# A two-layer hybrid block: ten input chunks in one 512-column product, and softmax probabilities turned by 32x32 blocks and transfers

## The reference

```python
h = rms_norm(x, norm_mix[l])
proj = h @ w_in[l]
(dq, dk, dv, dz, da, db, mq, mk, mv, lx, ly, gates) = split_columns(proj)
# delta rule: q, k, v = split(silu(causal_depthwise_conv(concat(dq, dk, dv), conv_w)))
# recurrence: xc = causal_depthwise_conv(lx, conv_w) + conv_b
# attention, one block of 256 keys:
s = where(k_pos <= q_pos, q @ k.T * scale, -inf)
o = softmax(s) @ v
```

## Time and profile before

| | |
|---|---|
| median of 3 runs | 910.72 us |
| profiled execution | 911.29 us |
| its span | 909.5 us |
| TensorE matmul busy | 898.0 us, 99% |
| VectorE busy | 661.5 us, 73% |
| ScalarE busy | 513.9 us, 56% |
| granted TensorE clock over the span | 0.998 |
| bytes moved | 173.22 MB, 190 GB/s |

### The profile page before, as it was taken

How to read it: one execution, slowest core, us unless ns; L and a number is a source line. 1 busy time by engine, 2 the same in 40 slices (tenths; PEclk the granted TensorE clock), 3 DMA queues, 4 the chain that set the end, 5 groups by cost and what they waited for, 6 DMA issues and landing times.

```text
span 909.5 us, 13892 instructions
## 1 busy us (share of the span) xinstructions
PE 898.0 (99%) x5460; PEld 765.8 (84%) x5460; DVE 661.5 (73%) x1096; ACT 513.9 (56%) x877; POOL 2.4 (0%) x6
## 2 busy tenths in 40 slices
PE   8999999999999999999999999999999999999996
PEld 5999899788887888888879998988888888888885
DVE  6879876797968665656688797767978675665756
ACT  7586555875446444445465766568644554444443
POOL 0000000000000000000000000000000000000000
PEclk9999999999999999999999999999999999999999
DMA  8544435456664777677755344255656567767761
GB/s 308 196 157 163 146 112 162 162 197 231 206 224 158 214 200 255 201 220 250 216 179 171 117 163 138 96 181 190 229 192 205 184 215 216 252 196 231 237 202 47
DMA packets 99281, 173.22 MB, mean 190 GB/s; under 512 B 53136, under 2 KB 59024, under 8 KB 99216
## 3 DMA queue, kind: packets, MB, share of 16 engines
q1 hardware_dynamic: 98928, 172.26, 58.6%
q10 hardware_dynamic: 288, 0.08, 0.0%
HBM read 165.49 MB, written 6.82 MB: 189 GB/s over the span
## 4 chain that ended last, share of the span: by engine, by line
PE 93%; DVE 4%; ACT 1%; DMA 1%; issue 0%; SPq 0%; DVEq 0%; ACTq 0%
PE bank L542 7%; PE bank L444 7%; PE bank L445 7%; PE bank L446 7%; PE bank L543 7%; PE bank L544 7%; PE bank L347 5%; PE bank L348 5%; PE bank L349 5%; PE bank L619 5%; PE bank L386 5%; PE bank L387 5%; PE bank L388 5%; PE bank L375 2%; PE bank L376 2%; PE bank L374 2%
## 5 line engine op out<-in xcount | busy, mean ns | idle before, releaser
L877 ACT CAST whi<-raw 128x1024 fp32r<-128x1024 f32 x292 | 305.8, 1053 | 301.5 <-PE bank L446 94.9
L1217 DVE TENSOR_TENSOR wlo<-raw,whi 128x1024 fp32r<-128x1024 f32 x292 | 350.2, 1216 | 74.6 <-ACT whi L877 72.0
L347 PE MATMUL bank<-ahi,whi 128*128 128x256 f32 x448 | 129.6, 289 | 0.8 <-DVE tmp L1267 0.8
L348 PE MATMUL bank<-alo,whi 128*128 128x256 f32 x448 | 126.6, 283 | 0.0
L349 PE MATMUL bank<-ahi,wlo 128*128 128x256 f32 x448 | 126.6, 283 | 0.0
L542 PE MATMUL bank<-whi,ahi 128*128 128x512 f32 x288 | 114.4, 397 | 1.4 <-DVE small L1299 0.8
L544 PE MATMUL bank<-whi,alo 128*128 128x512 f32 x288 | 112.3, 390 | 0.0
L444 PE MATMUL bank<-whi,ahi 128*128 128x512 f32 x288 | 112.2, 390 | 0.0
L543 PE MATMUL bank<-wlo,ahi 128*128 128x512 f32 x288 | 112.2, 390 | 0.0
L446 PE MATMUL bank<-whi,alo 128*128 128x512 f32 x288 | 112.1, 389 | 0.0
L445 PE MATMUL bank<-wlo,ahi 128*128 128x512 f32 x288 | 112.0, 389 | 0.0
(11 more groups left out here) (270 smaller groups left out, 1301.2 us busy)
## 6 DMA issues: line engine op xcount, KB each, us to landing
raw<-stream_dram SPq DMA_DIRECT2D x292, 512.0 KB, 4.6
turned_dram<-proj SPq DMA_DIRECT2D x144, 32.0 KB, 1.7
proj<-turned_dram SPq DMA_DIRECT2D x18, 256.0 KB, 4.6
proj<-gbias_dram SPq DMA_DIRECT2D x12, 256.0 KB, 4.6
par<-params_dram SPq DMA_DIRECT2D x2, 556.5 KB, 7.5
x<-x_dram SPq DMA_DIRECT2D x2, 512.0 KB, 5.3
mixture_dram<-proj SPq DMA_DIRECT2D x16, 64.0 KB, 1.9
proj<-mixture_dram SPq DMA_DIRECT2D x2, 512.0 KB, 3.9
```

Source lines behind the costliest of these rows:

```text
L347: pe.matmul(dst, whi_of(m)[:, wcol], hi, start=first, stop=False, skip_group_check=True)
L348: pe.matmul(dst, whi_of(m)[:, wcol], lo, start=False, stop=False, skip_group_check=True)
L877: act.copy(whi_of(m), raw_of(m)).then_inc(*AC.up(("hi", m), "w"))
L1217: dv.tensor_tensor(wlo_of(m), raw_of(m), whi_of(m), ALU.subtract).then_inc(*DV.up(("lo", m), "w"))
```

## The change

There are three parts. First, ten of the fourteen input chunks (`SUMMED`) use one matmul of 512 columns for hi x hi and hi x lo together: the two activation parts lie side by side in a new tile `parts`, so the moving operand is both, and the result has the main sum in columns 0 to 255 of a bank and the small one in 256 to 511. The third product adds to the main half. The weights are laid out anew, so that a half chunk is 128 outputs over all 1024 input channels, and half n uses bank n. Chunks 6 to 9 (`COPIED`) keep three matmuls of 256 columns.

Second, the halves are added on leaving PSUM, one step after the half chunk is done: ScalarE copies the small half to SBUF, VectorE adds the main half to it, and the convolutions read the sum from SBUF. TensorE waits for that addition (`emptied`) before it uses the bank again, which is for the same half of the next chunk.

Third, TensorE's transposes of the probabilities go. VectorE transposes blocks of 32x32 (step 36), SP stores in four transfers and loads the turned probabilities (its steps 40 and 41), and `pv` moves from step 37 to 42. The products behind move as well: the recurrence's second gate product from 42 to 45 and its chain by three steps (last step 60 instead of 57), the delta rule's output transposes from 42 to 43, one product of the state from 34 to 35.

```diff
+SUMMED = CONVS + LX + (14, 15)
+COPIED = (6, 7, 8, 9)
...
-        ahi = sb("ahi", [P, KT, T], F32R)
-        alo = sb("alo", [P, KT, T], F32R)
+        parts = sb("parts", [P, KT, 2, T], F32R)
+        ahi, alo = parts[:, :, 0, :], parts[:, :, 1, :]
...
-        def in_bank(c):
-            return bank[FM.index(c) % 2]
-
-        def in_copied(c):
-
-            if c in CONVS:
-                return DV, ("conv", CONVS.index(c))
-            if c in LX:
-                return DV, ("xc", LX.index(c))
-            return AC, ("in", c)
+        def in_tile(c, n):
+
+            return 56 + 2 * (CONVS.index(c) % 2) + n if c in CONVS else 2 * c + n
+
+        def emptied(c, n):
+            return (DV, ("sum", c, n)) if c in SUMMED else (AC, ("in", c, n))
+
+        def finished(chunks, k):
+
+            return [(c, n) for c in chunks for n in range(2) if AT[c] + 1 + n == k]
...
+                    if k == 40:
+                        sp.wait_ge(*DV.at(l, "probs32"))
+                        for a in range(4):
+                            sp.dma_start(probs.rearrange("b c (g q) -> c g b q", q=P)[:, :, :, 32 * a:32 * a + 32],
+                                         flat(tiles(PT, 6, slice(32 * a, 32 * a + 32))).rearrange("c (g b k) -> c g b k", g=12, b=4)
+                                         ).then_inc(written_probs, 16)
+                    if k == 41:
+                        sp.wait_ge(written_probs, 64 * (l + 1))
+                        sp.dma_start(flat(tiles(PR, 6)), probs.rearrange("b c n -> (b c) n")).then_inc(loaded_probs, 16)
...
-            def by_output(l, k, dst, start_kt):
-
-                for i in range(4):
-                    kt = start_kt + i
-                    for n in range(2):
-                        ins = products(dst[:, n * T:(n + 1) * T], cols(2 * i + n), l * NH + k,
-                                       ahi[:, kt, :], alo[:, kt, :], kt == 0 and n == 0, kt == KT - 1)
+            def by_output(l, k, c, n):
+
+                m, main = l * NH + k, bank[n][:, 0:T]
+                for kt in range(KT):
+                    if c in SUMMED:
+                        pe.matmul(bank[n][:, :], whi_of(m)[:, cols(kt)], flat(parts[:, kt, :, :]), start=kt == 0, stop=kt == KT - 1, skip_group_check=True)
+                        ins = pe.matmul(main, wlo_of(m)[:, cols(kt)], ahi[:, kt, :], start=False, stop=kt == KT - 1, skip_group_check=True)
+                    else:
+                        ins = products(main, cols(kt), m, ahi[:, kt, :], alo[:, kt, :], kt == 0, kt == KT - 1)
                 ins.then_inc(*PE.up(("bulk", k)))
...
-                if k == 35:
-                    pe.wait_ge(*DV.at(l, "probs"))
-                    pe.wait_ge(*AC.at(l, "state"))
-                    pr = flat(tiles(PR, 6))
-                    for g in range(12):
-                        ins = pe.transpose(b3((2, 3, 5)[g // 4], 4)[:, g % 4, :], pr[:, g * P:(g + 1) * P], ident[:, :])
-                    ins.then_inc(*PE.up("pT"))
-                if k == 37:
-                    pe.wait_ge(*AC.at(l, "pcopy"))
-                    vt, pt = wide(VTOK, 4), wide(PT, 6)
+                if k == 42:
+                    pe.wait_ge(loaded_probs, 16 * (l + 1))
+                    pe.wait_ge(*AC.at(l, "tanh_i"))
+                    vt, pt = wide(VTOK, 4), wide(PR, 6)
...
-                if k in (40, 42):
+                if k in (40, 45):
                     w = "wi" if k == 40 else "wr"
                     if k == 40:
                         pe.wait_ge(*DV.at(l, ("xc", 1)))
+                        pe.wait_ge(*DV.at(l, "masked"))
+                    else:
                         pe.wait_ge(*DV.at(l, "mb_out"))
-                    else:
-                        pe.wait_ge(*AC.at(l, "tanh_i"))
...
-                        if n > 1 and half == 0:
-                            by, name = in_copied(FM[n - 2])
+                        if n:
+                            by, name = emptied(FM[n - 1], half)
                             pe.wait_ge(*by.at(l, name))
-                        by_output(l, k, bank[n % 2], 4 * half)
+                        by_output(l, k, FM[n], half)
...
+                for c, n in finished(COPIED, k):
+                    rows = slice(32 * (2 * (c % 2) + n), 32 * (2 * (c % 2) + n) + 32)
+                    act.wait_ge(*PE.at(l, ("bulk", k - 1)))
+                    act.copy(proj[:, in_tile(c, n), :], bank[n][:, 0:T]).then_inc(*AC.up())
+                    act.copy(proj[rows, ROT + 2 * (c // 8), :], bank[n][rows, 0:T]).then_inc(*AC.up(("in", c, n)))
+                for c, n in finished(SUMMED, k):
+                    act.wait_ge(*PE.at(l, ("bulk", k - 1)))
+                    if c in CONVS[2:]:
+                        act.wait_ge(*DV.at(l, ("conv", CONVS.index(c) - 2)))
+                    act.copy(proj[:, in_tile(c, n), :], bank[n][:, T:2 * T]).then_inc(*AC.up(("small", c, n)))
                 if k in CONV_AT:
                     c = CONV_AT.index(k)
-                    act.wait_ge(*PE.at(l, ("bulk", k - 1)))
                     if c >= 2:
                         act.wait_ge(*DV.at(l, ("silu", c - 2)))
                     for i in range(2):
-                        act.activation(tmp[:, c % 2, i * T:(i + 1) * T], in_bank(CONVS[c])[:, i * T:(i + 1) * T], ACT.Copy,
+                        act.wait_ge(*DV.at(l, ("sum", CONVS[c], i)))
+                        act.activation(tmp[:, c % 2, i * T:(i + 1) * T], proj[:, in_tile(CONVS[c], i), :], ACT.Copy,
                                        scale=p_("conv", TAPS * (2 * CONVS[c] + i) + 3)).then_inc(*AC.up(("tap", c)))
                 if k in (AT[12] + 2, AT[13] + 2):
                     c = CHUNK[k // 2 - 1]
-                    act.wait_ge(*PE.at(l, ("bulk", k - 1)))
                     if c == 12:
                         act.wait_ge(*PE.at(l, "scores"))
                     for i in range(2):
                         t = 2 * (c - 12) + i
-                        act.activation(proj[:, XC + t, :], in_bank(c)[:, i * T:(i + 1) * T], ACT.Identity, bias=p_("convb", t),
+                        act.wait_ge(*DV.at(l, ("sum", c, i)))
+                        act.activation(proj[:, XC + t, :], proj[:, in_tile(c, i), :], ACT.Identity, bias=p_("convb", t),
...
-                if k in (AT[6] + 2, AT[7] + 2, AT[8] + 2, AT[9] + 2, AT[14] + 2, AT[15] + 2):
-                    c = CHUNK[k // 2 - 1]
-                    act.wait_ge(*PE.at(l, ("bulk", k - 1)))
-                    if c < 10:
-                        for i in range(2):
-                            rows = slice(32 * (2 * (c % 2) + i), 32 * (2 * (c % 2) + i) + 32)
-                            act.copy(proj[rows, ROT + 2 * (c // 8), :], in_bank(c)[rows, i * T:(i + 1) * T]).then_inc(*AC.up(("rows", c)))
-                    act.copy(flat(tiles(2 * c, 2)), in_bank(c)[:, :]).then_inc(*AC.up(("in", c)))
...
-                if k == 36:
-                    act.wait_ge(*PE.at(l, "pT"))
-                    for i in range(3):
-                        act.copy(flat(tiles(PT + 2 * i, 2)), bank[(2, 3, 5)[i]][:, :]).then_inc(*AC.up("pcopy"))
-                if k == 38:
+                if k == 43:
...
+                for c, n in finished(SUMMED, k):
+                    dv.wait_ge(*AC.at(l, ("small", c, n)))
+                    step(dv.tensor_tensor(proj[:, in_tile(c, n), :], bank[n][:, 0:T], proj[:, in_tile(c, n), :], ALU.add), ("sum", c, n))
...
-                    conv(l, [in_bank(CONVS[c])[:, i * T:(i + 1) * T] for i in range(2)], [tmp[:, c % 2, i * T:(i + 1) * T] for i in range(2)],
+                    conv(l, [proj[:, in_tile(CONVS[c], i), :] for i in range(2)], [tmp[:, c % 2, i * T:(i + 1) * T] for i in range(2)],
...
+                if k == 36:
+                    dv.wait_ge(*DV.at(l, "probs"))
+                    for i in range(3):
+                        step(dv.transpose(flat(tiles(PT + 2 * i, 2)), flat(tiles(PR + 2 * i, 2))), "probs32")
...
-    wi = _columns(turned).reshape(L, KT, P, C_IN, 256).transpose(0, 3, 2, 1, 4).reshape(L, C_IN, P, 2 * HALF)
+    wi = _columns(turned).reshape(L, KT, P, C_IN, 2, P).transpose(0, 3, 2, 4, 1, 5).reshape(L, C_IN, P, 2 * HALF)
```

More of the change, by code:

```diff
@@ L599, in gate_tokens @@
                         else:
-                            pe.wait_ge(*(AC.at(l, ("in", 15)) if t else DV.at(l, ("xc", 1))))
+                            pe.wait_ge(*DV.at(l, ("sum", 15, t)))
                     ins = token_half(l, k, q, t, gate_bank(e, t)[:, :])
@@ L754, in side @@
                     ins.then_inc(*PE.up("ks"))
+                if k == 35:
                     for h in range(HEADS):
@@ L1539, in side @@
                     r = ROT + 2 * (k == 23)
-                    dv.wait_ge(*AC.at(l, ("rows", 7 if k == 13 else 9)))
+                    dv.wait_ge(*AC.at(l, ("in", 7 if k == 13 else 9, 1)))
                     step(dv.stream_shuffle(proj[:, r + 1, :], proj[:, r, :], [(i + 16) % 32 for i in range(32)]), ("shuffle", k == 23))
@@ L1549, in side @@
```

(6 more changed lines are left out.)

45 lines of the change are left out of this document (23 added, 22 removed).

## The result

The changed kernel took 928.91 us (median of four runs, 926.8 to 931.32) against 910.75 for the kernel before on the same chip: 1.0194 of before, 95% interval 1.0181 to 1.0206. That is slower by 1.9%, or 18.2 us, where I forecast 9.5, and just outside my range of 911 to 928.

A forecast was written before the change was run, and what follows sets the result against it. TensorE's stream of columns was taken as the bound. A layer: -3.81 us for what goes, +8.55 for waits, so +4.74; two layers +9.5, giving 920 us, with an 8-in-10 range of 911 to 928.

The forecast's parts named there:

- step 10: Input projection: VectorE's addition stands between two weight splits, so TensorE waits 0.4 us a layer.
- step 19: Input projection: chunk 1's second-half addition stands behind a weight split ending at 75.36; TensorE waits 2.85 us a layer.
- steps 26 and 27: Last chunk's convolution starts later; TensorE waits about 1.3 us for ScalarE's copy of X, 0.2 ahead of it.
- step 35: Addition delayed by VectorE's chain with ScalarE's exponentials: TensorE waits 0.4 us.
- step 36: Gate product waits for the addition behind the split: 2.1 us, then another 1.3 for its second half.
- step 20: TensorE's old wait of 0.42 us a layer for the convolution goes.
- The transposes: Twelve softmax transposes leave TensorE: 1.25 us a layer saved, 2.5 in all.
- A: Whole kernel: all waits hidden, only the gains stay, 903 us; chance 0.05.
- B: The wait at step 19 is the only one, 908.8 us; chance 0.07.
- D: 512-column matmuls take 131 ns, TensorE saves 35 us, VectorE then bounds, about 890 us; chance 0.01.
- rival C: Slower still: transfer over 18 us, up to 3 us a layer, 926; also lower clock after waits; chance 0.13.
- the gain of the products: Input projection: merged 512-column products save 0.107 us a step, 2.14 a layer, 4.3 in all.

The follow-up runs named there:

- e1: Kernel before with only the transfer of the probabilities added (VectorE transposes, stores, load, products moved); input products unchanged: 909.93 us, 0.9977 of before.
- e4: Kernel after with useless 512-column products ahead of two waits a layer, 12 before step 19's and 7 before step 36's: 923.89 us, 1.0133 of before.
- e8: e7 with each 512-column product made as two of 256 into the same bank: 916.25 us, 1.0047 of before.
- e12: Kernel before run once more, unchanged, for a second trace of layer 0's last group: 910.96 us, one run.
- e3: Kernel after with one addition a layer moved: chunk 1's second half is added within VectorE's step 17: 923.71 us, 1.0130 of before.
- e6: Kernel after with four additions a layer moved earlier, and chunk 1's gate multiplication one weight split earlier: 916.52 us, 1.0051 of before.
- e7: e6 with one more move: in step 26 ScalarE copies X before it scales chunk 5: 915.88 us, 1.0043 of before.
- e9: Kernel after with four additions a layer moved earlier and chunks 1, 4, 14 and 5 back to three products without additions: 911.63 us, 1.0002 of before.
- e2: Kernel after with the probabilities transposed on TensorE as before; 512-column products and additions stay: 928.24 us, 1.0180 of before.

## Why the prediction was right in direction and wrong in size

**Right.** The bound and the mechanism: VectorE's addition empties the bank one step later, and TensorE waits for it. The places and most sizes: 0.41 at step 10 (forecast 0.4), 3.1 to 3.2 at step 19 (2.85), 1.52 at steps 26 and 27 (1.5 for the waits), 0.42 at step 35 (0.4), 1.84 and 1.90 at the first half of step 36 (2.1), 0.99 at its second half in layer 1 (1.3). The wait for the convolution at step 20 went. The transposes gave 1.20 a layer (1.25). The stores and load cost nothing on TensorE (e1). Rivals A and B are refuted by the waits, D by the pair: 0.35 us and not 0.25. Two slips in the working decided nothing. For steps 35 and 36 its own figures give 2.8 us and not 2.5: the bank free at 143.9 + 1.1 + 0.35, TensorE ready at 144.24 - 1.25 - 0.43. And its last paragraph calls the pair 0.348 where the sum has 0.3467.

**Wrong: the wait at step 19 was priced by its length alone** ("Wait: 2.85 us a layer"), and so was the one at step 36. I knew the other part. It stood in rival C as "waits of 2 to 3 us are new", with the lower level of 1.2 GHz costing "as much again", and I gave it 0.13 beside my own case. But my own case contained those waits, so the clock belonged in its sum, weighted by its chance, and not in a rival. In the profile it is worth, at step 20, 0.93 + 0.42 and 2.13 + 0.42 (the old wait being gone), and behind step 36 of layer 0 the difference between the layers, 4.54 - 2.58 and 0.57 - 0.12: 6.3 us. e4's trace gives the same 6.3, its runs 5.0 to 5.6. That is the larger part of what I missed.

**Too large: the gain of the products**, forecast 2.14 a layer. The sum of the step shifts without waits is about 1.2, and e8 has 0.065 a step where I had 0.107. The failed number is 0.2267 for a matmul of 512 columns. It came from a stream in which all have 512. Before one of 256 it takes 0.234 (mean of 290 in the trace after), and the one behind it 0.116: 0.3505 a pair, against 3 x 0.1198. That leaves 0.071 a step and explains 1.4 us of the shortfall. By the step shifts the shortfall is 1.8 us over both layers; the last 0.4 is not explained.

**Not forecast:** 1.55 us from step 47 of layer 0 to its end, from a wait in its last group (open, e12), and 0.6 more at step 19. With 6.3 and 1.8 they make 10.3 of the 10.5 us between my +9.5 and the profile's +20.0.

**A gap in the reasoning that the total hides.** I treated each wait as a place. From step 18 to 29 they are one chain: in each of the moves tried one wait went and another of 1.1 to 1.7 us appeared (e3, e6, e7), until additions were removed (e9). My 2.85 at step 19 was about right for this order of instructions. It would have misled for a repair: moving that addition took a wait of about 3 us away and gave back 1.2 us a layer, clock apart.

## What to carry to other kernels

Price a new wait of TensorE twice: its length, and the products behind it at half clock. A cause that the likeliest case contains belongs in its sum, not beside it.
Work handed to an engine is judged by its busy share in the stretch where the other engine will wait for it, before the change (here 18.69 of 20 us), not over the span (73%). There the reorderings tried moved the wait more than they shortened it, and only less work removed it. Elsewhere order can matter more: in steps 34 to 37 it gave back 2.5 us a layer of 3.9.
A merged operation is worth its spacing in the stream that it will stand in: here 0.065 us a step, and nothing where TensorE waits anyway.

## What the runs showed of the hardware that I had not expected

The lower clock is not certain behind a wait of one length. At step 19 it fell in both layers of the kernel after, behind waits of 3.06 and 2.96 us, and in only one of e2's, behind 3.07 and not behind 3.24. At step 36 it fell behind 1.84 us in layer 0 and not behind 1.90 in layer 1, and there only about 1 us into the work behind the wait: matmuls at 150.92 and 151.15 are 0.23 us apart, those from 151.38 on 0.39 and more. The four runs of the kernel after go with it: 926.8 us at a mean clock of 0.994, 928.44 and 929.39 at 0.991, 931.32 at 0.989. They spread over 4.5 us, those of e1, with clocks of 0.997 to 0.999, over 1.6. The wait in the last group varies too, so the clock need not be all of it.
